# A layer trunk on one core: first loads reordered, weight pieces split as they land, retention's decay exponents moved, one turn of the odd layer a block later

## What is computed

```
mod = silu(c) @ ada_w[layer] + ada_b[layer]      # ada_w[layer]: 1024 x 3072
shift, scale, gate = split(mod)
h = rmsnorm(x, pre_g) * (1 + scale) + shift
```

## Time and profile before

| | us |
|---|---|
| median of 3 runs | 2371.25 (2369.34 to 2372.03) |
| profiled execution, its own time | 2368.78 |
| its span, first to last instruction | 2366.7 |
| mean granted clock of TensorE | 0.989 of full |
| PE busy | 2257.7 (95% of the span) |
| DVE, ACT, POOL busy | 1406.8, 1139.5, 1028.1 |

### The profile page before, as it was taken

How to read it: one execution, slowest core, us unless ns; L and a number is a source line. 1 busy time by engine, 2 the same in 40 slices (tenths; PEclk the granted TensorE clock), 3 DMA queues, 4 the chain that set the end, 5 groups by cost and what they waited for, 6 DMA issues and landing times. The chain is left out here.

```text
span 2366.7 us, 34587 instructions
## 1 busy us (share of the span) xinstructions
PE 2257.7 (95%) x11426; PEld 1895.1 (80%) x11426; DVE 1406.8 (59%) x2145; ACT 1139.5 (48%) x2147; POOL 1028.1 (43%) x763
## 2 busy tenths in 40 slices
PE   4999998999998999999999989998999999999998
PEld 3788887888887778777777868887888888877886
DVE  6333335434344777777777751215899999984342
ACT  3544434222223655555555545556555566653332
POOL 5422222222222433333232242322998999982454
PEclk8999999999999999999999999999999999999999
DMA  8334423343434534343333233331111211253653
GB/s 297 134 136 147 142 94 134 123 149 120 151 126 132 156 96 116 92 111 92 108 97 103 61 132 127 121 133 36 45 50 49 67 58 40 76 177 108 178 159 108
DMA packets 196117, 271.15 MB, mean 115 GB/s; under 512 B 10532, under 2 KB 137764, under 8 KB 191398
## 3 DMA queue, kind: packets, MB, share of 16 engines
q1 hardware_dynamic: 191398, 261.43, 34.6%
q10 hardware_dynamic: 4608, 8.39, 0.9%
HBM read 183.27 MB, written 86.51 MB: 114 GB/s over the span
## 5 line engine op out<-in xcount | busy, mean ns | idle before, releaser
L2338 POOL TENSOR_TENSOR conv_g<-conv_g,product 128x1024 f32<-128x1024 f32 x160 | 384.8, 2407 | 34.3 <-ACT product L2387 24.6
L2485 DVE SCALAR_TENSOR_TENSOR ps_b<-u,cols,ps_b 128x1024 f32<-128x1024 f32 x304 | 391.6, 1288 | 9.2
L2601 PE MATMUL ps_a<-ho_hi,wp_lo 128*128 128x512 f32 x768 | 300.6, 391 | 6.8 <-DVE h_left L2541 6.8
L2602 PE MATMUL ps_a<-h_left,wp_hi 128*128 128x512 f32 x768 | 299.8, 390 | 0.0
L2603 PE MATMUL ps_a<-ho_hi,wp_hi 128*128 128x512 f32 x768 | 299.6, 390 | 0.0
L2387 ACT ACTIVATE product<-u,cols 128x1024 f32<-128x1024 f32 x160 | 183.3, 1151 | 169.7 <-POOL conv_g L2338 168.4
L1590 ACT ACTIVATE pt_hi<-ps_pt 128x512 fp32r<-128x512 f32 x256 | 154.5, 604 | 198.9 <-PE ps_pt L1786 198.7
L1701 DVE TENSOR_TENSOR pt_lo<-ps_pt,pt_hi 128x512 fp32r<-128x512 f32 x256 | 175.6, 686 | 119.7 <-ACT pt_hi L1590 114.9
L1645 POOL TENSOR_TENSOR v_lo<-v_st,v_hi 128x512 fp32r<-128x512 f32 x64 | 84.2, 1316 | 236.9 <-DVE v_hi L1677 236.9
L1691 DVE TENSOR_REDUCE mx<-ps_s 128x1 f32<-128x512 f32 x248 | 166.9, 682 | 23.2 <-PE ps_s L1778 22.2
L2601 PEld LDWEIGHTS ps_a<-ho_hi,wp_lo 128*128 128x128 f32 x768 | 144.8, 189 | 38.6 <-DVE h_left L2541 8.7
(11 more groups left out here) (445 smaller groups left out, 5619.0 us busy)
## 6 DMA issues: line engine op xcount, KB each, us to landing
scratch_ret_pack<-pack SPq DMA_DIRECT2D x14, 1280.0 KB, 5.5
pack<-scratch_ret_pack SPq DMA_DIRECT2D x14, 1280.0 KB, 6.6
k_st<-scratch_k_t SPq DMA_DIRECT2D x64, 256.0 KB, 3.5
v_st<-scratch_v SPq DMA_DIRECT2D x64, 256.0 KB, 3.7
ada<-in_ada_w_dram SPq DMA_DIRECT2D x16, 768.0 KB, 6.4
wp_raw<-in_od_w_in_dram SPq DMA_DIRECT2D x24, 512.0 KB, 3.9
xt<-in_x_dram SPq DMA_DIRECT2D x16, 512.0 KB, 6.1
ada<-in_ada_w_dram SPq DMA_DIRECT2D x8, 1024.0 KB, 7.8
```

The source lines that it names most:

```text
L2338: pool.tensor_tensor(half(conv_g, h), half(conv_g, h), product[adds(c, i, h) % 2][:], ALU.add).then_inc(added, 1)
L2485: dve.scalar_tensor_tensor(acc[h], units(c, k, h), params(c, k), acc[h], ALU.mult, ALU.add).then_inc(tap, 1)
L2601: pe.matmul(dst, lo[:, k, :], h_hi[:, k, t], start=k == 0, stop=False)
L2602: pe.matmul(dst, hi[:, k, :], h_lo[:, k, t], start=False, stop=False)
```

## The change

In words: (1) SP issues the four pieces of column block 0 of the weights between the `ada` pieces 5 to 7 instead of behind them, each with a semaphore of its own, and ACT splits each as it lands. (2) DVE's eight exponent instructions for `decay`, its Exp and its scaling leave setup; they are done in project_retention behind tile 1 (the sums on DVE, the Exp on ACT) and ahead of tile 14 (the scaling). For this `lg` moves to the store that lives through the kernel, 32 bytes a partition. (3) DVE takes `w_lo` k = 1, 2 and 3 directly behind its last `ada` sum, POOL keeps k = 0. (4) Tile 1 of x is squared and normalised in setup, and goes from project_retention. SP no longer waits for its landing, ACT does. (5) In odd_in the turn of `nt` moves from slot 90 to slot 91 on PE and so from slot 89 to 90 on ACT, and the split of `m_t` from slot 91 to 92.

```
 setup, SP:
             for k in range(KD):
                 if k >= NW:
+                    load_w(0, k - NW, w0_in[k - NW])
                     sp.wait_ge(mod_sum, k - NW + 1)
                 sp.dma_start(ada[:, place(k), :], ada_view[k][:, 0:2 * D]).then_inc(ada_in[place(k)], 16)
-            for j in range(3):
-                if j == 1:
-                    sp.dma_start(xt[:, 1, :], x_pieces[1]).then_inc(x_ahead[1], 16)
+            load_w(0, 3, w0_in[3])
+            sp.dma_start(xt[:, 1, :], x_pieces[1]).then_inc(x_ahead[1], 16)
+            for j in range(1, 3):
                 for k in range(KD // 2):
-                    sp.dma_start(w_raw[:, 2 * k:2 * k + 2, j * BANK:(j + 1) * BANK],
-                                 w_view[k][:, :, j * BANK:(j + 1) * BANK]).then_inc(w_in[j], 16)
-            sp.wait_ge(x_ahead[1], 16)
+                    load_w(j, k, w_in[j])
 setup, ACT:
             act.wait_ge(e_ready, 1)
-            act.activation(st.decay[:], expo[:], ACT.Exp)
...
-            act.wait_ge(w_in[0], 64)
             for k in range(KD // 2):
                 at = slice(2 * k, 2 * k + 2), slice(0, BANK)
+                act.wait_ge(w0_in[k], 16)
                 act.activation(w_hi[:, *at], w_raw[:, *at], ACT.Copy).then_inc(whi_done, 1)
+            act.wait_ge(x_ahead[1], 16)
+            act.wait_ge(x0_turned, 1)
+            act.activation(sq, xt[:, 1, :], ACT.Square, accum_out=ssq[1][:]).then_inc(sq_done, 1)
             act.wait_ge(red_step, 5)
             act.activation(st.sin[:].rearrange("p t f -> p (t f)"), red[:, 0, :], ACT.Sin)
             act.activation(st.cos[:].rearrange("p t f -> p (t f)"), red[:, 1, :], ACT.Sin)
+            act.wait_ge(rstd_done, 2)
+            act.activation(xn[:], xt[:, 1, :], ACT.Copy, scale=rstd[1][:])
 setup, POOL (norm(i): the two small instructions that make rstd of tile i):
-            for k in range(2):
-                at = slice(2 * k, 2 * k + 2), slice(0, BANK)
-                pool.wait_ge(whi_done, k + 1)
-                pool.tensor_tensor(w_lo[:, *at], w_raw[:, *at], w_hi[:, *at].bitcast(F32), ALU.subtract)
+            pool.wait_ge(whi_done, 1)
+            pool.tensor_tensor(w_lo[:, 0:2, 0:BANK], w_raw[:, 0:2, 0:BANK], w_hi[:, 0:2, 0:BANK].bitcast(F32), ALU.subtract)
+            norm(1)
 setup, DVE:
-                for h in range(H):
-                    f, b = lg[:, h:h + 1], lg[:, H + h:H + h + 1]
-                    step(dve.tensor_scalar(expo[:, h, :], table(C_FWD, P), f, None, ALU.mult))
-                    step(dve.scalar_tensor_tensor(expo[:, h, :], table(C_BWD, P), b, expo[:, h, :],
-                                                  ALU.mult, ALU.add))
...
-                dve.tensor_scalar(st.decay[:], st.decay[:], float(DK) ** -0.5, None, ALU.mult)
...
-                if k == NPE + 1:
-                    folds()
...
+            folds()
+            for k in range(1, KD // 2):
+                at = slice(2 * k, 2 * k + 2), slice(0, BANK)
+                dve.wait_ge(whi_done, k + 1)
+                dve.tensor_tensor(w_lo[:, *at], w_raw[:, *at], w_hi[:, *at].bitcast(F32), ALU.subtract)
             dve.wait_ge(mod_first, 1)
             step(dve.tensor_reduce(mods_pe[:], ...))
-            dve.wait_ge(whi_done, 3)
-            dve.tensor_tensor(w_lo[:, 4:6, 0:BANK], ...)
...
-            dve.wait_ge(whi_done, 4)
-            dve.tensor_tensor(w_lo[:, 6:8, 0:BANK], ...)
 project_retention, ACT:
             split_w(1)
-            norm(1, 1, 0)
             split_w(2)
...
             step(1, 1, 0)
+            act.wait_ge(decay_sums, 2 * H)
+            act.activation(st.decay[:], st.decay[:], ACT.Exp).then_inc(decay_exp, 1)
 project_retention, POOL:
             split_w(1)
-            rstds(1, 1)
             split_w(2)
 project_retention, DVE:
             step(1, 1, 0)
+            for h in range(H):
+                dve.tensor_scalar(st.decay[:, h, :], st.table[:, 0:P], st.lg[:, h:h + 1], None, ALU.mult).then_inc(decay_sums, 1)
+                dve.wait_ge(decay_sums, 2 * h + 1)
+                dve.scalar_tensor_tensor(st.decay[:, h, :], st.table[:, C_BWD - C_FWD:C_BWD - C_FWD + P], st.lg[:, H + h:H + h + 1],
+                                         st.decay[:, h, :], ALU.mult, ALU.add).then_inc(decay_sums, 1)
...
+            dve.wait_ge(decay_exp, 1)
+            dve.tensor_scalar(st.decay[:], st.decay[:], float(DK) ** -0.5, None, ALU.mult)
 odd_in:
-        TURN_V, TURN_N, TURN_V1 = NSLOT - 8, NSLOT - 6, NSLOT - 3
+        TURN_V, TURN_N, TURN_V1 = NSLOT - 8, NSLOT - 5, NSLOT - 3
 odd_in, ACT:
                 if s == NSLOT - 5:
                     next_w(range(0, 3))
+                if s == NSLOT - 4:
                     act.wait_ge(o.m_done, 1)
                     act.activation(o.m_hi[0][:], o.m_t[:], ACT.Copy).then_inc(o.mhi_done, 1)
-                if s == NSLOT - 4:
                     next_w(range(3, KD))
```

More of the change, by code:

```diff
@@ L131, in open_store @@
     st.tail = sb("tail", [P, 8])
+    st.lg = sb("lg", [P, 2 * H])
     st.early_at = nc.sbuf_base
@@ L173, in setup @@
         logit = sb("logit", [P, 2 * H])
-        lg = sb("lg", [P, 2 * H])
+        lg = st.lg
         tiny = sb("tiny", [P, 8, 2 * H])
-        expo = sb("expo", [P, H, P])
         expw = sb("expw", [P, 2 * H])
@@ L184, in setup @@
         sq = xn[:]
-        ssq, ms, rstd = [sb(f"{n}_x0", [P, 1]) for n in ("ssq", "ms", "rstd")]
+        ssq, ms, rstd = [[sb(f"{n}_x{i}", [P, 1]) for i in range(2)] for n in ("ssq", "ms", "rstd")]
         dec_ps = ctx.enter_context(nc.psum_tensor("dec_ps", [P, BANK], F32))
@@ L210, in setup @@
         xn_done = sem("xn_done0")
+        x0_turned = sem("x0_turned")
+        w0_in = [sem(f"w0_in{k}") for k in range(KD // 2)]
         ident = st.const[:, C_ID:C_ID + P]
@@ L249, in _ @@
             act.wait_ge(x_ahead[0], 16)
-            act.activation(sq, xt[:, 0, :], ACT.Square, accum_out=ssq[:]).then_inc(sq_done, 1)
+            act.activation(sq, xt[:, 0, :], ACT.Square, accum_out=ssq[0][:]).then_inc(sq_done, 1)
             act.wait_ge(rstd_done, 1)
-            act.activation(xn[:], xt[:, 0, :], ACT.Copy, scale=rstd[:]).then_inc(xn_done, 1)
+            act.activation(xn[:], xt[:, 0, :], ACT.Copy, scale=rstd[0][:]).then_inc(xn_done, 1)
             act.wait_ge(e_ready, 1)
-            act.activation(st.decay[:], expo[:], ACT.Exp)
             act.activation(st.q_w[:], expq[:], ACT.Exp)
@@ L268, in _, with norm @@
             pool.memset(st.neg_half[:], -0.5).then_inc(ms_done, 1)
[L269 to L272, removed]
+            def norm(i):
+                pool.wait_ge(sq_done, i + 1)
+                pool.tensor_scalar(ms[i][:], ssq[i][:], 1.0 / D, EPS, ALU.mult, ALU.add).then_inc(ms_done, 1)
+                pool.wait_ge(ms_done, i + 2)
+                pool.tensor_tensor(rstd[i][:], ms[i][:], st.neg_half[:, 0:1], ALU.pow).then_inc(rstd_done, 1)
+            norm(0)
             pool.wait_ge(pos_ready, 1)
@@ L307, in _ @@
             for k in range(KD):
-                pe.transpose(ps_h[k // 4][:, (k % 4) * P:(k % 4 + 1) * P], xn[:, k * P:(k + 1) * P], ident)
+                mm = pe.transpose(ps_h[k // 4][:, (k % 4) * P:(k % 4 + 1) * P], xn[:, k * P:(k + 1) * P], ident)
+            mm.then_inc(x0_turned, 1)
             pe.wait_ge(c_ready, 1)
@@ L394, in _ @@
                 ins.then_inc(mod_sum, 1)
+            folds()
[3 more added lines that the diff above has]
+                dve.tensor_tensor(w_lo[:, *at], w_raw[:, *at], w_hi[:, *at].bitcast(F32), ALU.subtract)
             dve.wait_ge(mod_first, 1)
             step(dve.tensor_reduce(mods_pe[:], mod_ps[:, 0:2 * KD * NPE].rearrange("p (m k) -> p m k", k=NPE), AX.X, ALU.add))
-            dve.wait_ge(whi_done, 3)
-            dve.tensor_tensor(w_lo[:, 4:6, 0:BANK], w_raw[:, 4:6, 0:BANK], w_hi[:, 4:6, 0:BANK].bitcast(F32), ALU.subtract)
             for m in range(4):
@@ L409, in _ @@
                                      st.cols[:, K_PRE + layer * KD:K_PRE + (layer + 1) * KD], ALU.add, ALU.mult)
-            dve.wait_ge(whi_done, 4)
-            dve.tensor_tensor(w_lo[:, 6:8, 0:BANK], w_raw[:, 6:8, 0:BANK], w_hi[:, 6:8, 0:BANK].bitcast(F32), ALU.subtract)
 def project_retention(nc, st, x, xt, xn, ps_h, w_hi, w_lo, w_raw, w_in, h_hi, h_lo, pack, ahead, ada_w):
@@ L474, in project_retention @@
         ht_first = sem("ht_first")
+        decay_sums = sem("decay_sums")
+        decay_exp = sem("decay_exp")
         hi_first = sem("hi_first")
@@ L562, in outs @@
                 act.activation(pack[s][:, RP_Q:RP_Q + BANK], ps_t[:], ACT.Copy).then_inc(t_out, 1)
-            act.sem_inc(ss_ready, 1)
-            act.sem_inc(xn_ready, 1)
+            act.sem_inc(ss_ready, 2)
+            act.sem_inc(xn_ready, 2)
             def split_w(j):
@@ L625, in split_w @@
                                        ALU.subtract).then_inc(wlo_done[j - 1], 1)
-            pool.sem_inc(ms_ready, 1)
-            pool.sem_inc(rstd_ready, 1)
+            pool.sem_inc(ms_ready, 2)
```

(2 more changed lines are left out.)

3 lines of the change are left out of this document (added).

## The result

The changed kernel takes 2357.04 us, median of 5 executions (2355.62 to 2362.24), against 2371.25 (2368.65 to 2372.07, 5 executions): ratio 0.9947, 95% interval 0.9933 to 0.996, so faster by 14.2 us, 0.5%. The forecast was 2355.8. The profiled execution took 2355.62 us with a span of 2353.8; before it was 2366.7, so 12.9 us are to be found, where the prediction's sum had 15.4. The near hit of the median hides a miss: the term for odd_in came out at 0.8 us where the sum had 4.4.

A forecast was written before the change was run, and what follows sets the result against it. PE, in work 95% of the span, was taken as the bound, so only its waits or half clock could give time. 7.6 + 1.5 + 1.4 + 0.5 + 4.4 = 15.4 us off 2371.25 gave 2355.8, range 2351.5 to 2360.5.

The forecast's parts named there:

- term 2: End of odd_in: PE gains 4.4 us (3 to 6.3), after a new 1.8 us wait at slot 93 for `vt[1]`.
- Setup, the loads: Setup: without the decay exponents the DMA queue stays full and the last `ada` sum ends at 34.2 instead of 38.7 us.
- Setup, the splits: Setup: DVE, held by POOL until about 36.0, ends its subtractions at 39.5; `ht` at 43.8, 7.6 us earlier.
- Rival (b): Setup's gain comes only in part, `ht` at 47 to 49 us, sum 11, time 2360; chance 0.19.
- Retention, first tiles: First tiles of retention: PE's waits go, gaining 1.5 us at tile 1's x, 1.4 at g, 0.5 at tile 2.
- The 1.5 at the turn of tile 1: Retention: tile 1's x is already normalised, so PE turns it at once; 1.5 us gained.
- The 0.5 at tile 2: Retention: tile 1's work on ACT, DVE and POOL moves earlier by more than PE, so PE's 0.54 us wait goes.
- The decay pieces: Retention: the moved decay instructions, up to 7 us on DVE, fit into waits for PE and cost 0.
- The sum: Whole kernel: all gains together 15.4 us, median from 2371.25 to 2355.8 us; chance 0.60.
- Rival (a): odd_in: the turn at slot 93 finds `vt[1]` landed; gain 17.3 us, time 2353.9; chance 0.13.
- (c): New waits take back PE's earlier start and odd_in's wait moves whole to slot 93; sum below 4.7 us; chance 0.05.
- (d): Slower: operands shifted 32 bytes by `lg` are read slower in retention's 16 tiles; 18 us slower, 2389; chance 0.03.

The follow-up runs named there:

- e4: Changed kernel with the decay exponents, their Exp and their scaling back in setup: 2364.74 us, ratio 0.9969 to the kernel before.
- e3: Changed kernel with block 0's four weight pieces loaded behind all `ada` pieces: 2358.61 us, ratio 0.9947 to the kernel before.
- e10: Changed kernel with `vt[1]` turned one slot later, block 0's weights behind all `ada` pieces, and all four setup subtractions on DVE: 2348.27 us.
- e2: Changed kernel with the turn of `vt[1]` one slot later (94 instead of 93): 2354.04 us, ratio 0.9928 to the kernel before.
- e9: The changed kernel run once more, with no edit: 2360.01 us, ratio 0.9946 to the kernel before.
- e5: Changed kernel with the gate stores of slots 90 and 91 placed behind ACT's first three copies of w_out: 2355.76 us, one execution.

## Why the prediction came out as it did

**Setup, the loads: right.** The hole at 20 us went, the last sum ended at 33.56 where 34.2 was forecast. e4 shows the cause: with the exponents back it ends at 39.15.

**Setup, the splits: right, the hold by POOL included.** The subtractions ended at 39.2, forecast 39.5, and `ht` came at 43.48, forecast 43.8. The sum was right in its end though not in each piece: the lock held DVE by more (2.2 us, not 1.6). What the `w` pieces cost the sums (1.9 us in e3, 3.8 in e10, charged 3.9) is not settled and did not decide: from POOL's start at 33.54 the four subtractions ran one after another. Rival (b), setup's gain in part, is out.

**Retention, first tiles: 2.5 us of waits instead of 3.4, and 0.5 by another way.** The 1.5 at the turn of tile 1 came whole. At g 1.0 came of 1.4: the step said that block 2's low parts end 15.6 us after `ht`, since ACT waits less; they end 17.3 after (60.80), because the eight subtractions of blocks 1 and 2 now come in one row and go one at a time. The lock that the prediction charged in block 0 it left out here. The 0.5 at tile 2 did not come. The step laid it to tile 1's work on three engines; DVE's timeline shows another thing just ahead of `h_lo`:

```profile
86.30 0.49 DVE L706 TENSOR_SCALAR gate<-gate_w,silu_c 128x512 f32<-128x512 f32 x1 [11.08 <-DMA gate_w<-in_ada_w_dram]
86.71 1.22 DVE L655 TENSOR_TENSOR h_lo<-ht,h_hi 128x1024 fp32r<-128x1024 f32 x1
```

DVE stands 11 us for the load of `gate_w`, in before too, ends `h_lo` at 87.93 and PE starts at 87.98. SP issues that load in the loop (75.46 us after, 86.41 before), so it moves with the loop, and the 0.54 stays. This is read from the traces; no run moved the load. In its place came 0.5 us that the step had excluded ("at PE's half clock too"): PE's matmuls reach full pace 4.0 us after it starts on tile 0 and not 4.9 (50.55 against 59.31, starts 46.54 and 54.45). So the stretch from `ht` to the MLA stage is 3.0 us shorter.

**The decay pieces: right,** cost 0, with 2.4 us where up to 7 were allowed for; e4 without them is no faster from `ht` to the MLA stage.

**odd_in: the mechanism right, term 2 mis-sized.** The new wait was foreseen at its place and for its load. PE reached it 17.2 us after the first `w_last`, forecast 17.35, and the load was issued 12.6 after, forecast 12.4. What failed is the landing "6.7 us later": it was 8.6, and the 6.7 was taken over from an execution in which one gate store, and not three, lay between w_out's first piece and the load. That makes the wait 4.0 instead of 1.8, and behind 4.0 us the clock fell, 1.7 us more: 4.4 - 1.9 - 1.7 = 0.8. The prediction had each as a reason for its lower bound of 3, half clock or a landing 1 us later, and not that the one brings the other, so the bound was too high. e2 shows the term at its full size, 6.6, when the wait is gone.

**The sum.** 7.9 + 1.5 + 1.0 + 0.5 + 0.8 = 11.7 us against 15.4; with the 1.2 of the middle the profiles differ by 12.9, and the medians by 14.2. That the forecast is within 1.3 us of the median is in part luck: 2.5 of the 14.2 us lie in no edited stretch. On another chip the changed kernel had 2360.01 and the kernel before 2372.53, 12.5 us apart. Rival (a), the tile landed in time, was wrong in direction; of (c) the half came true that the wait moves to slot 93 with half clock, but setup's gain stood. Of (d), slower operands at the shifted addresses, no trace shows a sign: DVE's rope instructions of tile 1 last 0.69 and 0.68 us in both kernels.

## What to carry to other kernels

A load's time to land belongs in part to what the DMA queues hold at that moment (8.6 us here with the gate stores ahead, 6.0 with idle DMA engines): when a change moves PE earlier, list what else moves ahead of the load (stores of the engine that waited for PE above all), and take the wait with its clock as one event, not two. When two engines hold each other off an operand port, the sum of their durations is the time, in every place where they meet; give the work to the faster one. If what a gain hangs on is 1 to 5 us, measure it by a stretch between two unchanged instructions, since 1740 us of unchanged code varied by 8.

## What the runs showed of the hardware

- Waits of PE of 1.06, 2.28, 2.62 and 2.74 us near the end of odd_in left the clock at 1.00; waits of 3.44, 3.50, 3.60 (twice), 3.64, 4.01, 4.96 and 5.06 us were followed by a clock of 0.50. Each time 1.7 us of pace were lost (1.5 in before): in e9, for one, the five microseconds behind the turn of `vt[1]` have 1.00, 0.54, 0.50, 0.50 and 0.76.
- A DMA on ACT's queue that stands in the program behind ACT's copies went out beside the first of them (e5: 2113.10 and 2113.09): a place in ACT's program is not a time.
- The Exp of the decay pieces, now inside project_retention, brought a table load of 1.28 us, and the compiled program loads a table again in later tiles of the loop, twice in each pass (12 loads from 94.80 to 294.33; none in e4 after its 72.28). They hide in ACT's waits for PE. ACT's timeline after, the first and one of the later ones:

```profile
91.45 1.28 ACT L599 ACT_TABLE_LOAD   x1
...
132.83 1.28 ACT L552 ACT_TABLE_LOAD   x1 [6.30 <-PE ps_h L746]
142.18 1.28 ACT L567 ACT_TABLE_LOAD   x1
```

- In e10 POOL's angle instructions with one operand, beside DVE's four subtractions, lasted 2.89 and 2.16 us instead of 1.94 and 1.50, and DVE's four 5.45 instead of 4.62: the hold is not only between subtractions.
